# Order of the weight splits, head scalings and key turns in the input projection of a one-core decoder step

## The chip, the cores and the metric

The kernel runs as one program on one core of a Trainium2 chip. The metric is the device time of one execution in microseconds (us), as the median of a few runs. Engines are named as in the profile: PE (matmul), PEld (its weight loads), DVE (VectorE), ACT (ScalarE), POOL (GpSimd), SP (the engine whose queue issues the DMAs).

## The reference, cut to what matters

The reference is one inference step of a two-layer hybrid decoder over 1024 prompt tokens and 64 sample tokens. The change touches only the first stage of layer 0, the combined input projection with what hangs on it:

```
xn = rmsnorm(x, norm_mix[0])
h  = einsum('btd,de->bte', xn, w_in)             # 1088 rows x 3400 columns
qa, ka, va, qi, ki, wi, hb = split(h)
q_a = rmsnorm(qa per head, a_q_norm)             # also k_a and each q_b, k_b
dots = einsum('bqhd,bsd->bqhs', qi, ki) * IDX_DIM**-0.5
sc   = einsum('bqh,bqhs->bqs', wi, relu(dots))   # index scores
_, idx = top_k(sc, 256)                          # the keys that sparse attention sees
```

A head's rmsnorm is a sum of squares, a root, a reciprocal, a product with the reciprocal, and a product with a gain row of 64 values. The bias of every softmax comes from a table of 32 buckets by 20 heads, spread out over distances.

## The kernel before, in words

`stage_project` takes the first 459 us of the 2642 us span. Everything behind it (window attention, sparse attention, output projection, MLP, the recurrent layer, the second MLP) is code that the change does not touch. A block ends with a barrier of all engines, so the next stage begins when the last engine of this one is through.

The 3400 columns are cut into 8 groups (`GROUPS`, L56): group 0 is "kikv" (index keys, index weights, keys, values), 1 "qi" (index queries), 2 "qa", 3 to 5 "qk0" to "qk2", 6 and 7 values. The 1088 rows are 9 tiles (tile 0 is the 64 sample rows). The pair (group, tile) is called a step here, as (3,5). `rows_n` numbers the steps: n = 9 x group + tile.

Each fp32 product is made of three passes over high and low parts. A weight unit is the 128 x 512 piece k of a group (8 to a group). It is loaded by SP into a ring of three raw buffers (`load_w`, L517, waits until the low part three units back is made), its high part is made by a DVE cast (`split_high`, L967), its low part by a POOL subtraction (`split_unit_low`, L612). PE begins a group when all 8 low parts are there (L807).

A tile's way is: PE `project` (L818, three PSUM banks in turn, so PE can be three tiles ahead of ACT); ACT copies the bank to a row buffer, scaled (L748; a ring of three, so the copy of step n waits until the rows of step n-3 have been stored by DMA); ACT squares (L770); DVE sums (L998); ACT root (L695), issued one tile later; DVE reciprocal and product (`norm_apply`, L1014), also a tile later; POOL head gain (L661); SP `store` (L544), two tiles later in its queue. In the groups that aren't stored (1) or not normed (6, 7) steps drop out. Tile 0 of the later groups is projected together with its low part, and POOL adds the two halves (`add_first`, L640).

In group 0 seven tiles are projected together. Behind (1,0) PE makes the bias table (six chunks, L899; the last two need the banks back that ACT takes first), ACT takes it in six copies (`take_table`, L713) when all its copies of group 0 are done, SP writes it to memory (L557, L559) and then writes strips of it (`bias_halves` to `bias_strips`, L564, five of them, the first two of 2 MB), with loads of weights and the stores of (0,7) and (0,8) between them in SP's order. After (1,1) PE turns the index keys by transposes in one PSUM bank, in three parts with an ACT copy between them (L910, L754), then the sample queries (`turn_queries(0)`, L835, which waits for `add_first(1)`), and after (1,4) the queries of tile 2 (`turn_queries(2)`, L839), which wait for ACT's copy of (1,3). Index scores follow, mixed with the projection.

From group 2 on ACT and DVE find the top 256 of each row by bisection over 31 bits, spread over the tile steps: `show` (L292, four ACT sign passes with sums) and `turn` (L303, L310, L312, tiny DVE operations) need each other's results in turn, in 3 of 4 steps. DVE ends with `settle` and `close` (L322 to L359), one piece after the other. The units of groups 3 to 7 stand at fixed steps in `WEIGHTS_AT` (L484 to L489), and DVE, POOL and SP all work down the same list of steps.

## Time and profile before

| | us |
|---|---|
| time, median of 3 runs | 2646.19 (2646.01 to 2652.25) |
| the profiled execution | 2644.74 |
| its span, first to last instruction | 2641.8 |
| PE busy in the span | 2533.1 (96%) |
| DVE, ACT, POOL busy in the span | 1560.0, 1050.5, 1246.4 |
| granted TensorE clock, mean | 0.979 |
| projection stage, end of PE's last matmul to start of the next stage's first | 455.84 to 459.24 |

The busy shares are means over stages with different limits; the projection stage has to be read by its stretches. A wait row says which engine or DMA ended the idle time of an engine.

### The profile page before, as it was taken

To read this page: it belongs to the slowest core of one execution; us is meant where nothing else is said; L and a number is where in the kernel's file an instruction comes from. 1 tells how busy PE (TensorE), PEld (TensorE's weight loads), DVE (VectorE), ACT (ScalarE), POOL (GpSimd) and SP (SyncE) were. 2 spreads that over 40 slices of the span, in tenths; PEclk is the share of its full clock that TensorE was granted. 3 is DMA by queue.
4 is the path that set the end of the run, shared out by engine and by line. 5 is a ranking of instruction groups with operands and counts; after the bars stand their busy time and mean duration, and the time that the engine had idled before them with its cause. 6 is when DMAs were issued, how large, how long until landed. Compare 5 with 4: busy or idle time off the path is not lost.

```text
span 2641.8 us, 44709 instructions
## 1 busy us (share of the span) xinstructions
PE 2533.1 (96%) x16674; PEld 2350.2 (89%) x16674; DVE 1560.0 (59%) x2510; ACT 1050.5 (40%) x1883; POOL 1246.4 (47%) x833
## 2 busy tenths in 40 slices
PE   7999999989879999999999989998999999999998
PEld 6667778866669999999999979998999999999998
DVE  5369886436555555545554697565355645554557
ACT  5358784866532332233223242435222233223322
POOL 4114451017335665556555583323455466545655
PEclk9999999989889999999999999999999999999999
DMA  5402222734461111111111112233111111111112
GB/s 151 137 21 77 82 84 84 233 91 117 152 228 48 41 56 48 40 48 56 48 33 46 48 33 82 75 114 140 43 40 57 40 41 55 48 40 48 56 48 84
DMA packets 109203, 198.71 MB, mean 75 GB/s; under 512 B 22709, under 2 KB 62773, under 8 KB 108805
## 3 DMA queue, kind: packets, MB, share of 16 engines
q1 hardware_dynamic: 104602, 191.85, 23.0%
q10 hardware_dynamic: 4480, 5.27, 0.6%
q8 instruction: 73, 1.20, 0.2%
q14 instruction: 48, 0.39, 0.1%
HBM read 170.97 MB, written 47.17 MB: 83 GB/s over the span
## 4 chain that ended last, share of the span: by engine, by line
PE 66%; DVE 3%; issue 1%; ACT 1%; POOL 1%; DMA 0%; DVEq 0%; ACTq 0%
PE d_ps L2322 40%; PE d_ps L2849 24%; PE d_ps L3211 1%; PE d_ps L2337 1%; DVE rstd_all L2409 0%; DVE x_t L2953 0%; DVE xg_low L3339 0%; DVE x_t L2944 0%; DVE xg_low L2348 0%; POOL m_hidden_low L2692 0%; DVE m_hidden L2897 0%; PE d_ps L2382 0%; DVE unit_high L2305 0%; POOL unit_low L2309 0%; DVE m_shared_part L2944 0%
## 5 line engine op out<-in xcount | busy, mean ns | idle before, releaser
L2322 PE MATMUL d_ps<-xg_high,unit_high 128*128 128x364 f32 (+1 forms) x2112 | 472.6, 332 | 9.0 <-DVE xg_low L3339 3.1
L2322 PE MATMUL d_ps<-xg_high,unit_low 128*128 128x364 f32 (+1 forms) x2112 | 464.8, 328 | 0.0
L2322 PE MATMUL d_ps<-xg_low,unit_high 128*128 128x364 f32 (+1 forms) x2112 | 464.4, 328 | 0.0
L2309 POOL TENSOR_TENSOR unit_low<-unit_raw,unit_high 128x1024 fp32r<-128x1024 f32 x96 | 232.4, 2421 | 412.2 <-DVE unit_high L2305 231.1
L2849 PE MATMUL d_ps<-m_hidden_high,unit_high 128*128 128x272 f32 x1792 | 373.8, 290 | 14.2 <-DVE x_t L2944 8.9
L2322 PEld LDWEIGHTS d_ps<-xg_high,unit_high 128*128 128x128 f32 x2112 | 365.5, 188 | 15.6 <-issue 5.6
L2849 PE MATMUL d_ps<-m_hidden_high,unit_low 128*128 128x272 f32 x1792 | 370.9, 288 | 0.0
L2849 PE MATMUL d_ps<-m_hidden_low,unit_high 128*128 128x272 f32 x1792 | 370.6, 288 | 0.0
L2322 PEld LDWEIGHTS d_ps<-xg_high,unit_low 128*128 128x128 f32 x2112 | 367.0, 189 | 0.0
L2322 PEld LDWEIGHTS d_ps<-xg_low,unit_high 128*128 128x128 f32 x2112 | 365.3, 188 | 0.0
L2699 POOL TENSOR_TENSOR unit_low<-unit_raw,unit_high 128x512 fp32r<-128x512 f32 x128 | 176.8, 1382 | 390.3 <-ACT unit_high L2767 388.9
L2767 ACT ACTIVATE unit_high<-unit_raw 128x512 fp32r<-128x512 f32 x128 | 81.1, 633 | 567.9 <-PE d_ps L2849 358.1
L2944 DVE TENSOR_TENSOR x_t<-x_t,d_ps 128x544 f32<-128x544 f32 x320 | 227.1, 718 | 134.2 <-PE d_ps L2849 133.8
L2849 PEld LDWEIGHTS d_ps<-m_hidden_high,unit_high 128*128 128x128 f32 x1792 | 281.6, 189 | 16.0 <-issue 15.4
L2849 PEld LDWEIGHTS d_ps<-m_hidden_high,unit_low 128*128 128x128 f32 x1792 | 283.6, 189 | 0.0
L2849 PEld LDWEIGHTS d_ps<-m_hidden_low,unit_high 128*128 128x128 f32 x1792 | 281.1, 188 | 0.0
L2692 POOL TENSOR_TENSOR m_hidden_low<-m_hidden,m_hidden_high 128x544 fp32r<-128x544 f32 x160 | 250.8, 1591 | 23.1 <-ACT m_hidden_high L2756 23.1
L2897 DVE SCALAR_TENSOR_TENSOR m_hidden<-d_ps,rstd_all 128x1092 f32<-128x1092 f32 x64 | 82.5, 1292 | 293.8 <-PE d_ps L2322 293.7
L818 PE MATMUL proj_ps<-w_high,x_high 128*128 128x512 f32 (+2 forms) x464 | 178.9, 386 | 2.8 <-ACT rows L748 2.6
L818 PE MATMUL proj_ps<-w_low,x_high 128*128 128x512 f32 (+2 forms) x464 | 175.7, 379 | 0.0
L818 PE MATMUL proj_ps<-w_high,x_low 128*128 128x512 f32 (+2 forms) x464 | 175.4, 378 | 0.0
L2761 ACT ACTIVATE unit_high<-unit_raw 128x1024 fp32r<-128x1024 f32 x60 | 63.6, 1060 | 250.6 <-PE d_ps L2849 127.3
(398 smaller groups left out, 4175.4 us busy)
## 6 DMA issues: line engine op xcount, KB each, us to landing
unit_raw<-w_units SPq DMA_DIRECT2D x160, 512.0 KB, 3.6
unit_raw<-w_in SPq DMA_DIRECT2D x48, 256.0 KB, 2.9
proj_rows<-rows SPq DMA_DIRECT2D x32, 256.0 KB, 2.0
s_win<-win_cache SPq DMA_DIRECT2D x2, 3968.0 KB
proj_rows<-rows SPq DMA_DIRECT2D x36, 128.0 KB, 1.8
sw_rows<-proj_rows SPq DMA_DIRECT2D x12, 384.0 KB, 4.7
select_work<-xt SPq DMA_DIRECT2D x8, 546.0 KB, 3.8
x_t<-xt SPq DMA_DIRECT2D x4, 1092.0 KB, 14.4
```

The source lines that it names most:

```text
L818: last = nc.tensor.matmul(ps[p % 3][:, 0:w], x, y[gi % 2][:, k, 0:w], start=(n == 0), stop=(n == len(passes) - 1))
L2309: self.nc.gpsimd.tensor_tensor(self.wl[slot][:, :], self.raw[:, slot, :], self.wh[slot][:, :].bitcast(F32), ALU.subtract).then_inc(self.w_ ...
L2322: last = self.nc.tensor.matmul(ps[:, c, 0:USED[c]], w[wslot][:, wk], v[:, k, c, 0:USED[c]], start=(k == 0 and n == 0), stop=(k == nk - 1 a ...
L2337: last = self.nc.tensor.matmul(ps[:, c, 0:USED[c]], w[wslot][:, wk], v[:, k, c, 0:USED[c]], start=(k == 0 and n == 0), stop=(k == nk - 1 a ...
L2692: nc.gpsimd.tensor_tensor(hl[:, i, q, :], SOURCES[i], hh[:, i, q, :].bitcast(F32), ALU.subtract).then_inc(h_low, 1)
L2699: nc.gpsimd.tensor_tensor(out, src, top.bitcast(F32), ALU.subtract).then_inc(part_low, 1)
L2761: nc.scalar.activation(d.wh[slot], d.raw[:, slot, :], ACT.Copy).then_inc(d.w_high, 1)
L2767: nc.scalar.activation(part_slots(d.high, x), src, ACT.Copy).then_inc(part_high, 1)
L2849: last = nc.tensor.matmul(out[:, c, :], w[:, i // 4, c0:c0 + P], h[:, i, q, HC * c:HC * (c + 1)], start=(i < 4 and q == 0 and x == 0), sto ...
L2897: nc.vector.scalar_tensor_tensor(out=v[:, t, :].rearrange("p (c n) -> p c n", c=NCH), in0=d.ps[t][:, :, 0:CH], scalar=0.0, in1=d.rstd[:, : ...
L2944: nc.vector.tensor_tensor(out, out, d.quarter[i], ALU.add).then_inc(added, 1)
L3211: last = nc.tensor.matmul(ps[use % 2][:, c, 0:CC], gw[:, n % 2, x, :], cv[:, n % 2, c, :], start=True, stop=True)
```

## The change

Four edits. `WEIGHTS_AT` puts the units k = 0 to 7 of groups 4 to 7 at steps -1, 0, 0, 1, 2, 2, 3, 4 of the group before (it was -1 to 6, one to a step). POOL does a step's low parts first and the head gain of an earlier tile behind them: two tiles behind in group 0, one from group 2 on (it was the gain of the same tile, which waited for DVE, ahead of the next low part). The last two gains of group 0 come at (1,0). One more unit of group 1 is loaded and split ahead (`FIRST_LOADS` 4, `FIRST_SPLITS` 3), which puts its load in SP's queue ahead of the load of the bias selector. The key turns use three PSUM banks and no wait between them; the sample queries are turned, and taken by ACT, one tile later; ACT takes the pending root of (0,8) before the table.

```diff
@@ -435,12 +435,16 @@
             return GROUPS[gi][1]
 
         WAVE = 7
-        FIRST_LOADS = 3
-        FIRST_SPLITS = 2
+        FIRST_LOADS = 4
+        FIRST_SPLITS = 3
 
         def table_bank(c):
 
             return pss[c // 2 % 2][:, 512 * (c % 2):512 * (c % 2) + 512]
+
+        def key_bank(t):
+
+            return pss[t - 1] if t else psx
 
         def bank(p):
 
@@ -486,7 +490,7 @@
             WEIGHTS_AT[k - AHEAD_3].append((3, k))
         for gi in range(4, NGR):
             for k in range(KD):
-                WEIGHTS_AT[NT * (gi - 3) + k - 1].append((gi, k))
+                WEIGHTS_AT[NT * (gi - 3) + (2 * k + 1) // 3 - 1].append((gi, k))
         SHOW_AT = {STEPS[1 + 4 * y // 3]: y for y in range(BITS + 1)}
         KEY_TURNS = [(0, TS + 3 * P), (TS + 3 * P, TS + 7 * P), (TS + 7 * P, TS + 8 * P)]
 
@@ -510,6 +514,7 @@
                 sp.wait_ge(S["filled"], 1)
                 sp.dma_start(relb[0:NBUCKET, :], a["rel_bias"]).then_inc(S["pick_in"], 16)
                 load_w(1, 2)
+                load_w(1, 3)
                 sp.wait_ge(S["x_squared"], KD)
                 sp.wait_ge(S["x_low"], KD)
                 sp.dma_start(pick, a["bias_pick"]).then_inc(S["pick_in"], 16)
@@ -639,27 +644,45 @@
                 v = st[0:TS, n % NST, 0:w]
                 nc.gpsimd.tensor_tensor(v, v, first_low[:, 0:w], ALU.add).then_inc(S["first_sum"], 1)
 
+            def gain_rows(gi, i):
+                for h0, hn, row, _ in kinds(gi):
+                    n = rows_n(gi, i)
+                    pool.wait_ge(S["normed"], NORM_AT[gi, i] + 1)
+                    v = st[:, n % NST, HD * h0:HD * (h0 + hn)].rearrange("p (h d) -> p h d", h=hn)
+                    nc.gpsimd.tensor_tensor(v, v, gains[:, row:row + 1, :].broadcast_to([P, hn, HD]),
+                                            ALU.mult).then_inc(S["gained"], 1)
+
+            def gain_late(gi, i, lag):
+                if NT * gi + i >= lag:
+                    gain_rows(*divmod(NT * gi + i - lag, NT))
+
             for gi in range(NGR):
                 for i in range(NT):
-                    if i == 0 and gi in (1, 2):
-                        add_first(gi)
-                    if i == NT - 1 and 2 <= gi < NGR - 1:
-                        add_first(gi + 1)
                     k = i + (FIRST_SPLITS if gi == 0 else 0)
-                    if gi < 2 and k < KD:
-                        split_unit_low(pool, gi + 1, k)
-                    if gi == 1 and i == NT - 1:
-                        for k in range(AHEAD_3):
-                            split_unit_low(pool, 3, k)
-                    if gi >= 2 and i < NT - 1:
-                        for unit in WEIGHTS_AT[NT * (gi - 2) + i]:
-                            split_unit_low(pool, *unit)
-                    for h0, hn, row, _ in kinds(gi):
-                        n = rows_n(gi, i)
-                        pool.wait_ge(S["normed"], NORM_AT[gi, i] + 1)
-                        v = st[:, n % NST, HD * h0:HD * (h0 + hn)].rearrange("p (h d) -> p h d", h=hn)
-                        nc.gpsimd.tensor_tensor(v, v, gains[:, row:row + 1, :].broadcast_to([P, hn, HD]),
-                                                ALU.mult).then_inc(S["gained"], 1)
+                    if gi == 0:
+                        if k < KD:
+                            split_unit_low(pool, 1, k)
+                        gain_late(0, i, 2)
+                    if gi == 1:
+                        if i == 0:
+                            gain_rows(0, NT - 2)
+                            gain_rows(0, NT - 1)
+                            add_first(1)
+                        if k < KD:
+                            split_unit_low(pool, 2, k)
+                        if i == NT - 1:
+                            for k in range(AHEAD_3):
+                                split_unit_low(pool, 3, k)
+                    if gi >= 2:
+                        if gi == 2 and i == 0:
+                            add_first(2)
+                        if i < NT - 1:
+                            for unit in WEIGHTS_AT[NT * (gi - 2) + i]:
+                                split_unit_low(pool, *unit)
+                        if (gi, i) != (2, 0):
+                            gain_late(gi, i, 1)
+                        if i == NT - 1 and gi < NGR - 1:
+                            add_first(gi + 1)
                 if gi >= 2:
                     for unit in WEIGHTS_AT[NT * (gi - 2) + NT - 1]:
                         split_unit_low(pool, *unit)
@@ -669,6 +692,8 @@
                         v = work[:, WORK_OFF[j] + P * j:WORK_OFF[j] + P * (j + 1)]
                         nc.gpsimd.affine_select(out=v, in_=v, compare_op=ALU.is_ge, fill=MASK, base=0,
                                                 pattern=[[-1, P]], channel_multiplier=1).then_inc(S["masked"], 1)
+
+            gain_rows(NGR - 1, NT - 1)
 
         def take_turn(act, j):
             act.wait_ge(S["turned"], TURN_Q[j])
@@ -718,6 +743,8 @@
                     p = NT * gi + i
                     w = width(gi)
                     if gi == 1 and i == 0:
+                        root(*pending)
+                        pending = None
                         take_table()
                     if gi == 1 and i - 3 in SEL_TILES:
                         for h in range(IH):
@@ -751,8 +778,8 @@
                         if i == 0:
                             for t, (x0, x1) in enumerate(KEY_TURNS):
                                 act.wait_ge(S["turned"], t + 1)
-                                nc.scalar.activation(kit[:, x0:x1], psx[:, 0:x1 - x0], ACT.Copy).then_inc(S["turn_taken"], 1)
-                        if i == 1:
+                                nc.scalar.activation(kit[:, x0:x1], key_bank(t)[:, 0:x1 - x0], ACT.Copy).then_inc(S["turn_taken"], 1)
+                        if i == 2:
                             act.wait_ge(S["turned"], TURN_Q[0])
                             nc.scalar.activation(
                                 qst[:, :, :].rearrange("d b (h t) -> d h b t", t=DT),
@@ -903,11 +930,10 @@
             pe.wait_ge(S["ms_dve"], 1)
             pe.wait_ge(S["tab_out"], 16 * 3)
             for t, (x0, x1) in enumerate(KEY_TURNS):
-                turn_free(t + 1)
                 for i in range(NT):
                     if x0 <= tile_col(i) < x1:
                         r = tile_rows(i)
-                        last = nc.tensor.transpose(psx[:, tile_col(i) - x0:tile_col(i) - x0 + r], kk[0:r, i, 0:P],
+                        last = nc.tensor.transpose(key_bank(t)[:, tile_col(i) - x0:tile_col(i) - x0 + r], kk[0:r, i, 0:P],
                                                    ident[0:r, 0:r])
                 last.then_inc(S["turned"], 1)
             for i in range(1, NT):
@@ -916,7 +942,7 @@
                     continue
                 if i > 1:
                     project(1, i)
-                if i == 1:
+                if i == 2:
                     turn_queries(0)
                 if i - 2 in SEL_TILES:
                     turn_queries(i - 2)
```

## Rows read from the trace of the kernel before

**Rows 1.** Windows: stretch, length; busy PE, PEld, DVE, ACT, POOL; clock; DMA.

```profile
98.00:193.00 95.00, 94.27 (x431) 58.22 (x432) 62.97 (x100) 45.75 (x72) 17.39 (x17) 1.00 0.17 48
193.00:412.00 219.00, 207.21 (x870) 164.74 (x869) 187.72 (x493) 180.76 (x353) 101.22 (x101) 0.98 0.27 82
```

**Rows 2.** Waits of PE, 46 to 98 us: line, releaser, total, times, longest.

```profile
PE proj_ps L818 <- POOL w_low L612: 6.9, 1, 6.9
PE turn_ps L835 <- POOL rows L640: 2.8, 1, 2.8
PE turn_ps L910 <- ACT late L754: 1.3, 2, 0.7
```

**Rows 3.** Windows of PE alone: length, busy, granted clock.

```profile
52.90:57.60 4.70, 4.62 (x11) 0.50 0.23 64
...
74.70:81.50 6.80, 4.21 (x16) 0.50 0.65 227
```

**Rows 4.** Timeline of ACT, 40 to 98 us: start, duration, what, idle before.

```profile
44.80 0.47 ACT L748 ACTIVATE rows<-score_ps,rstd_rows 128x256 f32<-128x256 f32 x1 [4.19 <-DMA proj_rows<-rows]
...
63.51 1.25 ACT L713 ACTIVATE late<-score_ps 20x512 f32<-20x512 f32 x2 [0.27 <-PE score_ps L899]
...
83.75 0.58 ACT L757 ACTIVATE sample_queries_t<-turn_ps 64x512 f32<-64x512 f32 x1
95.73 1.84 ACT L748 ACTIVATE rows<-proj_ps,rstd_rows 128x512 f32<-128x512 f32 x3 [11.40 <-DMA proj_rows<-rows]
```

**Rows 5.** Timeline of SP's queue, 54 to 86 us.

```profile
54.08 0.34 SPq L544 DMA_DIRECT2D proj_rows<-rows  x1
...
64.78 0.36 SPq L557 DMA_DIRECT2D bias_rows<-late  x1
...
85.79 0.52 SPq L544 DMA_DIRECT2D proj_rows<-rows  x1
```

**Rows 6.** Timeline of POOL: the last low part of group 1.

```profile
51.66 1.26 POOL L612 TENSOR_TENSOR w_low<-unit_raw,w_high 128x512 fp32r<-128x512 f32 x1
```

**Rows 7.** DMA issues on the page: KB each, us from issue to landing.

```profile
unit_raw<-w_in SPq DMA_DIRECT2D x48, 256.0 KB, 2.9
...
proj_rows<-rows SPq DMA_DIRECT2D x36, 128.0 KB, 1.8
```

**Rows 8.** Timeline of PE: the queries of tile 2.

```profile
97.05 0.66 PE L839 MATMUL turn_ps<-ident,rows 128*128 128x128 f32 x4 [0.33 <-ACT rows L748]
```

**Rows 9.** Waits of PE (193 to 412 us) for the low parts.

```profile
PE proj_ps L818 <- POOL w_low L612: 9.0, 2, 5.6
```

**Rows 10.** Waits of ACT for its row buffers, 197 to 412 us.

```profile
ACT rows L748 <- DMA proj_rows<-rows: 6.7, 8, 1.3
```

**Rows 11.** Timeline of ACT: the copies of (6,5) and (6,6).

```profile
414.38 0.69 ACT L748 ACTIVATE rows<-proj_ps,rstd_rows 128x512 f32<-128x512 f32 x1 [2.19 <-PE proj_ps L818]
419.95 0.69 ACT L748 ACTIVATE rows<-proj_ps,rstd_rows 128x512 f32<-128x512 f32 x1 [0.56 <-PE proj_ps L818]
```

**Rows 12.** Timeline of POOL: the gain of (5,8), then three low parts.

```profile
395.51 2.13 POOL L661 TENSOR_TENSOR rows<-rows,unit_raw 128x256 f32<-128x256 f32 x2 [0.63 <-DVE rows L1014]
397.61 2.45 POOL L612 TENSOR_TENSOR w_low<-unit_raw,w_high 128x256 fp32r<-128x256 f32 x3
```

**Rows 13.** Timeline of DVE: a cast that waits for its load.

```profile
400.77 0.29 DVE L967 CAST w_high<-unit_raw 128x256 fp32r<-128x256 f32 x1 [2.70 <-DMA unit_raw<-w_in]
```

**Rows 14.** DVE's last operation of the stage, and PE's first of the next.

```profile
457.66 0.69 DVE L359 TENSOR_SCALAR select_work<-late 128x1024 f32<-128x1024 f32 x1
...
459.24 0.63 PE L1631 MATMUL sw_ps_x<-ident,unit_raw 128*128 128x128 f32 x4 [3.40 <-PEq L371]
```

**Rows 15.** Timeline: a low part of POOL and a turn's operations on DVE.

```profile
256.12 1.28 POOL L612 TENSOR_TENSOR w_low<-unit_raw,w_high 128x512 fp32r<-128x512 f32 x1
...
256.21 1.22 DVE L310 TENSOR_SCALAR select_flip<-select_count 128x4 int32<-128x4 int32 x1
...
272.91 0.17 DVE L310 TENSOR_SCALAR select_flip<-select_count 128x4 int32<-128x4 int32 x1
```

## Prediction

> **What bounds the kernel now.** I read the page, then windows, waits and timelines of the projection stage, the only stage touched; all times are from the start of the span. Three limits follow each other in it.
>
> Up to 98 us it is a mixed chain. PE waits 6.9 us for the last low part of group 1, 1.3 us between the key turns and 2.8 us for the summed sample rows [rows 2], and its granted clock stands at 0.50, the 1.2 GHz level, from 52.9 to 57.6 and from 74.7 to 81.5 us [rows 3], each time after PE stood idle or nearly so. Beside it runs a DMA chain. When ACT has taken the table (its last two copies begin at 63.51 [rows 4]), SP writes it at 64.78 and then queues strips and weights, so that the store of (0,8) is issued at 85.79 [rows 5]. ACT's copy of (1,2) waits 11.40 us for that store and begins at 95.73; three copies follow back to back in 1.84 us [rows 4]. At 97.05 PE turns the queries of tile 2, after 0.33 us of waiting for the copy of (1,3) [rows 8]. PE and the DMA chain reach 97 us in a dead heat.
>
> From 98 to 193 us PE is busy for 94.27 of 95.00 us [rows 1]: what PE loses or gains before it reaches the bisection whole.
>
> From 193 to 412 us DVE is busy for 188 and ACT for 181 of 219 us [rows 1], bound to each other by show and turn. PE waits 9.0 us for low parts, at two starts of groups [rows 9], but ACT never waits for PE between 197 and 412 us: its copies stand idle for their row buffers only, 6.7 us [rows 10]. PE is up to three tiles ahead, and its stall is paid from that lead. Only at (6,5) and (6,6) does ACT wait for PE, 2.19 and 0.56 us [rows 11]. DVE ends the stage at 458.35 (its last operation starts at 457.66), and the next stage begins at 459.24 while PE has stood for 3.40 us [rows 14]. So PE's stalls of this part are worth 2.19 + 0.56 = 2.75 us at most, not 9.0.
>
> **The first low parts, group 1.** Now POOL makes the parts of k = 5, 6, 7 ahead of the gains of (0,0), (0,1), (0,2). The load of k = 5 now waits for the part of k = 2, which ends near 37.2, so it is issued near 37.6; with 2.9 us to land [rows 7] and the selector's transfer, now issued behind one more weight load, I take 42. The cast, the part (1.26 us [rows 6]) and the gain follow: gain of (0,0) near 44.2. The store lands 1.8 us later [rows 7], so ACT's copy of (0,3), at 44.80 before [rows 4], starts near 46.3. From it: square, sum, the gain's product, then the cast of k = 7 at 48.1 and its low part 48.6 to 49.9. It ended at 51.66 + 1.26 = 52.92 [rows 6]. PE starts group 1 some 3.0 us earlier.
>
> But the gain of (0,2) now stands behind that part, near 50.3, and each later copy of ACT waits for a store three tiles back. Copies of (0,5) and (0,6): 52.2 and 53.9. SP then issues the eight small loads behind the kiwi store of (0,6), and the store of (0,4) leaves near 57.4, where it left at 54.08 [rows 5]. Copies of (0,7) and (0,8) near 59.2 and 60.8, root of (0,8) 62.3, the table from 62.4. ACT takes it in six copies of about 0.6 (1.25 for two [rows 4]): done near 66.0, where it was 63.51 + 1.25 = 64.76. **Table +1.25 us.** PE's 3.0 us are lost to the two table chunks that need ACT's first copies. Bounds: with the copy of (0,3) at 45.0 the same chain gives -0.5, with 47.4 it gives +2.9.
>
> **The key turns.** Three banks take out the 1.3 us, the earlier root and the later sample queries the 2.8 us [rows 2], and the half clock there costs 4.21 / 2 = 2.1 us of PE [rows 3]. These 6 us are real, but they end in front of the turn of the queries of tile 2. That needs the copy of (1,3), which hangs on the store of (0,8), and SP's chain from table to store (64.76 to 95.7) isn't shortened by any edit: it moves by the +1.25. Moreover ACT takes the sample queries (0.58 us [rows 4]) now between the copies of (1,2) and (1,3): they were taken at 83.75, in a hole. **+0.6 us.** So PE reaches the turn near 91.3, stands some 7 us, and goes on near 98.9.
>
> **The clock behind that hole.** After the 6.9 us hole before, the half clock stayed for the 4.62 us of busy PE in the first window [rows 2, 3], which cost 4.62 / 2 = 2.3 us. The new hole is as long, and behind it lies the stretch where PE is the bound. I take **+2.0 us**; bounds 0 (the clock stays up) and 3.4 (6.8 us at half). Sum up to 193 us: 1.25 + 0.6 + 2.0 = +3.85.
>
> **Groups 2 to 7.** The low parts come early enough, and PE's 9.0 us of waiting turn into waiting for ACT's banks. ACT's last waits for PE go: **-2.75**. Against it, the gain of the last tile of a group now follows three low parts instead of none or one. For (5,8): gain 395.51 to 397.64, then three parts of 2.45 / 3 = 0.8 each [rows 12]; now the parts come first, from about 394.9, and the gain ends near 399.1. Store, the copy of (6,2) and the load of the next two units move with it, and the cast at 400.77 that already waited 2.70 us for its load [rows 13] comes near 402.2, ahead of a turn that ACT waits for: **+1.4** (bounds 0 to 2.1). For (4,8) the same order delays the gain by 1.2 us, of which I let half through: **+0.6** (0 to 1.2). The other two group ends move by under 0.5 us, into waits that exist. Doubled units cost DVE a cast of 0.4 us more in one step and less in another: 0.
>
> **Sum.** 3.85 - 2.75 + 1.4 + 0.6 = +3.1 us. The profiled execution took 2644.74 (span 2641.8), so it would take 2647.8; it lies 1.45 us under the median of the runs, so the median becomes 2646.19 + 3.1 = 2649.3. A difference of under 0.3%, about 8 us, can't be told from none here; this is one.
>
> **A lock between POOL and DVE.** A turn's 128 x 4 operation took 1.22 us when it started 0.09 us behind a low part of POOL, and 0.17 us without one [rows 15]. The change puts low parts directly behind the casts, and the turn is DVE's next operation. The Trainium skill ("SBUF — State Buffer", Who interferes with whom) says that GpSimd and VectorE share one pair of ports by a lock held for a whole instruction, and that issue order decides who is blocked. By that rule the trace agrees, and each part in front of a turn costs a part's length. In the sum I count 0, since before the change the parts ran behind a gain and hit the turns too (as this row shows), and the number of parts is the same.
>
> **Rivals.**
>
> A, the lock decides (slower). Of the eight doubled steps six have a turn; the second part blocks another of its operations. Four have parts of 512 columns, 1.22 - 0.17 = 1.05 us each, two parts of 256, 0.55 each: 5.3 us, if the two steps that lose their part in each group give nothing back. 3.1 + 5.3 = +8.4: 2654.6. For: show and turn are one loop with little idle. Against: DVE still waits for ACT in many steps. It decides when more than a third of the doubled steps pass their delay on.
>
> B, the front doesn't slip. The store of (0,0) lands early (table -0.5), the clock stays up or the strips run faster, and groups 6 and 7 keep their 2.75: -0.5 + 0.6 - 2.75 = -2.65: 2643.5. For: landing times are the softest numbers of my chain. Against: the store of (0,4) has SP's eight loads ahead in any case.
>
> C, PE was the bound of the whole stage after all (faster). If groups 2 to 7 alone pay it, the 9.0 us of waits go and, behind each of the two holes, at most the 2.3 us of half clock that the first hole cost: -13.6, 2632.6. With the front's 6.9 + 1.3 + 2.8 it would be -24.6. Against it stand ACT's copies that never wait for PE [rows 10].
>
> D, the edits do not do what they say: PE still waits for low parts of group 4, since casts of DVE are late. Then the -2.75 is missing: 2652.
>
> **How the numbers follow.** Forecast with D and its bounds (-0.5 to +7): 0.56. B: 0.24. A: 0.13. C: 0.07. Faster by over 0.3% is C and the rim of B: 0.09. Slower by over 0.3%: about two thirds of A and the case in which late landing (+2.9), clock (+3.4) and stalls (+3.3) meet: 0.13. The rest, 0.78, is within. Range: from B's far side, 2641, to just over A, 2657. The forecast's own range is 2645.5 to 2653.
>
> **What would show it.** Right: no PE wait for low parts from group 2 on; PE group 1 starts near 50; the table's last copy near 65; the store of (0,8) as many us behind it as before; an idle PE of 5 us or more in front of L839 near 98, with half clock behind it; ACT's waits for PE at (6,5) and (6,6) gone; a DVE cast that waits near 402. Wrong: a table before 64, no hole in front of the queries of tile 2, ACT waiting for PE between 200 and 400 us, or a DVE end more than 3 us before 458.

## The result: 9 us slower, of which the prediction had 3

The changed kernel took 2658.82 us (median of 8 runs, 2656.01 to 2663.64), the kernel before beside it 2652.69 (8 runs, 2646.01 to 2653.60). The ratio is 1.0034, 95% interval 1.0021 to 1.0048: 9.0 us, 5.6 to 12.7. Forecast were +3.1 us and 2649.3, with a range up to 2657.0. The sign was right; the size and the range were not. The base moved too: in five later jobs the kernel before had medians of 2648.84 to 2650.92 where the three runs of the prediction had 2646.19. On that base the measured 9.0 us would have given 2655.2, inside the range.

One profile of each kernel isn't enough here, because the kernel before alone differs from execution to execution. So each was profiled four times. Mean of four (lowest to highest), us from the start of the span:

| | before | after | difference | forecast |
|---|---|---|---|---|
| PE starts group 1 | 52.40 | 50.79 | -1.61 | -3.0 |
| ACT's table done | 65.70 (63.94 to 67.12) | 66.87 (66.50 to 67.41) | +1.17 | +1.25 |
| copy (1,2) to copy (1,3) | 0.58 | 1.06 | +0.48 | +0.6 |
| PE turns the queries of tile 2 | 98.46 (96.27 to 100.34) | 99.87 (99.54 to 100.58) | +1.41 | +1.85 |
| from there to ACT's copy (1,5) | 11.61 (11.57 to 11.65) | 14.45 (14.18 to 14.92) | +2.84 | +2.0 |
| copy (1,5) to the first show | 84.43 (84.40 to 84.47) | 88.26 (84.44 to 89.58) | +3.83 | 0 |
| first show to DVE's end | 265.11 (264.41 to 266.30) | 266.76 (266.65 to 267.02) | +1.65 | -0.75 |
| DVE's end to the next stage | 0.86 | 0.33 | -0.53 | 0 |
| start of the next stage | 460.47 | 469.67 | +9.20 | +3.1 |
| from there to the end of the span | 2187.6 | 2188.2 | +0.6 | 0 |

The 9.20 us at the start of the next stage agree with the 9.0 us of the ratio. The last row is code that the change doesn't touch, and it varies from 2182.5 to 2193.7 us between executions of either kernel: a single profile's span says nothing about 9 us. The table, too, is done at one of two times in the kernel before, near 64 (64.75 and 63.94) or near 67 (67.12 and 66.97), so the differences of means in the upper rows rest on how many of each kind the four were. The profile of after that was taken with the timed runs has a span of 2653.1 us, its execution 2656.01.

Its page: busy times of the engines.

```profile
PE 2542.2 (96%) x16674; PEld 2354.5 (89%) x16674; DVE 1567.5 (59%) x2510; ACT 1049.5 (40%) x1883; POOL 1242.8 (47%) x833
```

PE's waits of 46 to 99.8 us, answering [rows 2] (releaser; total, times, longest):

```profile
PE turn_ps L866 <- ACT rows L775: 6.5, 1, 6.5
PE proj_ps L845 <- POOL w_low L617: 4.1, 1, 4.1
PE score_ps L926 <- ACT late L738: 2.4, 1, 2.4
PE proj_ps L845 <- ACT rows L775: 1.0, 1, 1.0
```

The wait for the low part shrank from 6.9 to 4.1 us, those for the key turns and the summed sample rows are gone, and in their place stands the hole of 6.5 us ahead of the queries of tile 2.

The chain that made it, ACT's timeline after, answering [rows 4]:

```profile
47.17 0.47 ACT L775 ACTIVATE rows<-score_ps,rstd_rows 128x256 f32<-128x256 f32 x1 [3.85 <-DMA proj_rows<-rows]
...
66.12 0.52 ACT L738 ACTIVATE late<-score_ps 20x432 f32<-20x432 f32 x1 [0.85 <-PE score_ps L926]
...
97.93 0.69 ACT L775 ACTIVATE rows<-proj_ps,rstd_rows 128x512 f32<-128x512 f32 x1 [10.61 <-DMA proj_rows<-rows]
98.51 0.58 ACT L784 ACTIVATE sample_queries_t<-turn_ps 64x512 f32<-64x512 f32 x1
98.99 1.25 ACT L775 ACTIVATE rows<-proj_ps,rstd_rows 128x512 f32<-128x512 f32 x2
```

SP's queue after, answering [rows 5]: table, strips and weights still stand ahead of the stores of (0,7) at 75.13 and (0,8) at 88.64. Two of these instructions hold the queue for 3.70 and 9.10 us. The order isn't all of it: the store of (0,8) is seen as landed only at 97.84, 9.2 us after its issue, where such stores take 1.8 us at the median [rows 7].

```profile
66.66 0.36 SPq L562 DMA_DIRECT2D bias_rows<-late  x1
67.06 1.58 SPq L564 DMA_DIRECT2D bias_halves<-late  x2
70.51 0.78 SPq L569 DMA_DIRECT2D bias_strips<-bias_halves  x1
71.33 3.70 SPq L526 DMA_DIRECT2D unit_raw<-w_in  x1
75.13 0.67 SPq L549 DMA_DIRECT2D proj_rows<-rows  x1
76.78 1.80 SPq L537 DMA_DIRECT2D page_keys_t<-kidx_t  x2
78.62 0.76 SPq L569 DMA_DIRECT2D bias_strips<-bias_halves  x1
79.42 9.10 SPq L526 DMA_DIRECT2D unit_raw<-w_in  x1
88.64 0.53 SPq L549 DMA_DIRECT2D proj_rows<-rows  x1
```

PE after, answering [rows 8], and windows of PE (stretch, length; busy; granted clock, DMA share, GB/s), first the stretch behind the hole, then the one that nothing in the prediction had:

```profile
99.71 1.12 PE L866 MATMUL turn_ps<-ident,rows 128*128 128x128 f32 x4 [6.50 <-ACT rows L775]
```

```profile
96.40:106.60 10.20, 6.20 (x16) 0.50 0.47 146
181.80:195.50 13.70, 13.70 (x47) 0.50 0.15 39
```

The second stretch at the 1.2 GHz level lies over the sample scores (the index scores of the 64 sample rows), 64-row products without a wait of PE in front of them. They begin at 177.66 at full clock and end at 190.94; the clock falls in their midst, at 181.8. It holds back DVE, which stands until they are done. DVE in the kernel before, then after:

```profile
181.26 0.42 DVE L1069 COPY sample_work<-turn_ps 64x264 f32<-64x264 f32 x1 [6.18 <-PE turn_ps L932]
181.71 0.16 DVE L1071 TENSOR_TENSOR sample_work<-sample_work,later_mask 64x8 f32<-64x8 f32 x1
```

```profile
190.98 0.42 DVE L1095 COPY sample_work<-turn_ps 64x264 f32<-64x264 f32 x1 [10.40 <-PE turn_ps L958]
191.44 0.93 DVE L1097 TENSOR_TENSOR sample_work<-sample_work,later_mask 64x8 f32<-64x8 f32 x1
```

Between them lie 9.7 us: 5.5 were there at copy (1,5), the rest is this stretch. The operation behind the copy then took 0.93 us in place of 0.16, since it meets POOL's 1.27 us of adding rows, which began at 191.07 and ended at 192.34. In another execution of the same changed kernel neither is seen: there the copy waits 6.18 us again and the operation takes 0.16.

```profile
187.09 0.42 DVE L1095 COPY sample_work<-turn_ps 64x264 f32<-64x264 f32 x1 [6.18 <-PE turn_ps L958]
187.54 0.16 DVE L1097 TENSOR_TENSOR sample_work<-sample_work,later_mask 64x8 f32<-64x8 f32 x1
```

### The profile page after: what moved, and what is told of

It reads as the page before. It is cut to its first block, busy times and chain, and to the rows that moved or that the text cites. A ratio compares the mean times of both kernels' runs of the same rounds, so it can differ in the third digit from the quotient of the medians.

```text
span 2653.1 us, 44709 instructions
## 1 busy us (share of the span) xinstructions
PE 2542.2 (96%) x16674; PEld 2354.5 (89%) x16674; DVE 1567.5 (59%) x2510; ACT 1049.5 (40%) x1883; POOL 1242.8 (47%) x833
## 3 DMA queue, kind: packets, MB, share of 16 engines
HBM read 170.97 MB, written 47.17 MB: 82 GB/s over the span
## 4 chain that ended last, share of the span: by engine, by line
PE 66%; DVE 3%; issue 1%; ACT 1%; POOL 0%; DMA 0%; DVEq 0%; ACTq 0%
PE d_ps L2348 40%; PE d_ps L2875 24%; PE d_ps L3237 1%; PE d_ps L2363 1%; DVE rstd_all L2435 0%; DVE x_t L2979 0%; DVE x_t L2970 0%; DVE xg_low L3365 0%; DVE xg_low L2374 0%; DVE m_hidden L2923 0%; PE d_ps L2408 0%; DVE m_shared_part L2970 0%; DVE unit_high L2331 0%; POOL unit_low L2335 0%; DMA mixed_low<-mixed_t 0%
## 6 DMA issues: line engine op xcount, KB each, us to landing
x_t<-xt SPq DMA_DIRECT2D x4, 1092.0 KB, 14.2
```

## Experiments

"Half clock in the sample scores" below is the stretch just shown; its mark is the wait of DVE's copy, 10 us and more with it and 6.2 without. The kernel before that stood beside the runs of a job had a median of 2650.32 (e1 to e6), 2650.92 (e7, e8), 2648.84 (e9 to e12), 2650.72 (e13 to e16) and 2650.60 (e17, e18).

**The three parts one by one.** e1 keeps of the change only the groups' weights and late gains from group 2 on, e2 only the order of group 0, e3 only the key turns:

```diff
 e1, e2: as before
-                return pss[t - 1] if t else psx
+                return psx              # and turn_free(t + 1), root behind the table, queries at i == 1
 e1, e3: as before
-        FIRST_LOADS = 4; FIRST_SPLITS = 3; load_w(1, 3); gain_late(0, i, 2)
+        FIRST_LOADS = 3; FIRST_SPLITS = 2; gain_rows(0, i)
 e2, e3: as before
-                WEIGHTS_AT[NT * (gi - 3) + (2 * k + 1) // 3 - 1].append((gi, k))
+                WEIGHTS_AT[NT * (gi - 3) + k - 1].append((gi, k))   # and gain_rows(gi, i) in place of gain_late
```

> The kernel before with one part of the change only: from group 2 on, the units at 3 per two tiles and POOL's low parts ahead of the head gains of a tile before. My theory (the front costs, the back is nearly free because ACT and DVE pace it): PE's two waits for low parts of 9.0 us go, the first show starts at 193 us as before, settle begins within 2 us of 425.6 and DVE ends within 2 us of 458.3; time +0 to +2 us against before. Rival (the lock and the bunched parts slow the show and turn loop): first show at 193, but DVE ends 5 us or more later. Second rival (PE was the bound): DVE ends 5 us or more earlier, time -5 to -13.

> The kernel before with the order of group 0 only: four loads and three splits ahead, gains two tiles behind the low parts. My theory: PE starts group 1 near 50.7 instead of 53.0, but ACT's table copies end near 66.6 (64.8 before), SP's store of (0,8) and the copy of (1,2) come 2 us later (near 98), so PE turns the queries of tile 2 near 98.8 behind a hole of about 3 to 4 us; it loses 2 us there and up to 2 us of half clock behind the hole: +2 to +4 us at 120 us. Rival (the earlier low parts are a gain as they stand): PE passes 97 us on or before its time, time -2 us or better.

> The kernel before with the key turns in three banks, the root of (0,8) ahead of the table and the sample queries a tile later. My theory: PE's waits of 4.1 us and most of the half clock near 75 to 81 us go, but the copy of (1,2) still begins at 95.7, so a hole of about 5 us opens in front of the turn of the queries of tile 2, which comes at 97.5 (0.5 for the sample queries taken between the copies), with half clock behind it: +0.5 to +3.5 us at 120 us. Rival (the waits removed are on the path): PE is 4 us or more earlier at 97 us, time -4 us or better.

Measured: e1 2653.32 us, ratio 1.0011 (0.9998 to 1.0024); e2 2654.15, 1.0012 (0.9996 to 1.0027); e3 2658.39, 1.0036 (1.0022 to 1.0050). In e1 PE waits for no low part from group 2 on, only 10.0 us for ACT's rows, and the kernel isn't faster. In e2 the expected hole of 3 to 4 us didn't come: PE reaches the queries of tile 2 at 98.17 without waiting. The key turns alone are as slow as the whole change. In e3's profile the hole stands, though its table was done at 63.91, and 14.85 us go from the queries of tile 2 to copy (1,5) where e1 and e2 have 11.65. Windows of these stretches in e3 and in e2 show why:

```profile
97.00:111.90 14.90, 14.20 (x50) 0.73 0.45 132
```

```profile
98.20:109.80 11.60, 10.77 (x51) 1.00 0.45 123
```

The same work takes 3.3 us longer at a mean clock of 0.73. What PE gained ahead of the hole it didn't keep. Rival C, PE as the bound throughout, falls: e1 takes out the waits of groups 2 to 7 and e3 those of the key turns, and neither is faster.

**The stores ahead of the table.** e4 is the changed kernel with the stores of (0,7) and (0,8) issued by SP before it waits for the table; e8 moves three loads of group 2 ahead of it as well. e9 has the key turns alone with e4's stores.

```diff
                 if gi == 1 and i == 0:
+                    store(0, NT - 2)
+                    store(0, NT - 1)
+                    for k in range(3): load_w(2, k)      # e8 only
                     sp.wait_ge(S["tab_sb"], NTC)
```

> The changed kernel, with the stores of (0,7) and (0,8) issued in SP's queue ahead of the wait for the table instead of behind the strips. My theory (the hole of 6.5 us is the DMA queue's): copies of (1,1), (1,2), (1,3) no longer wait for DMA, PE turns the queries of tile 2 near 93 instead of 99.7 with no hole and full clock; but the second weight unit of group 2 lands near 97.5, so DVE's first scores start near 98 to 99 instead of 103.7. 4 to 8 us faster than the changed kernel up to 170 us. Rival (the hole belongs to something else, PE or ACT): the hole stays, time unchanged against the changed kernel. On the half clock of 181.8 to 195.5 us, in the sample scores: if it is a chance of phase, it stays in some of these four runs and not in others; if the change brings it, it stands in none of the first three.

> The changed kernel with the stores of (0,7) and (0,8) and the first three loads of group 2 issued ahead of the wait for the table. Against the kernel with the stores alone moved (turn of the queries at 92.4, but the copy of (1,5) at 105.6, 13.2 us behind it, since DVE's scores wait for the second unit): DVE's scores start with the first relu near 95, the copy of (1,5) comes near 104, 1 to 2 us earlier; first show near 189.5. Time 5 to 8 us under the changed kernel in its own fast runs, 1 to 3 under the kernel before. Rival (DMA isn't what the scores wait for): as with the stores alone.

> The kernel before with the change's edits to the key turns (three banks, the root early, the sample queries of tile 2 later) and the two stores of tile 7 and 8 of the first groups issued ahead of SP's wait for the table; the weights' parts and gains of the groups stay where they were before, and so does the order of the first group's projections. If the time of the change comes from the hole ahead of the queries of tile 2 and the half clock that follows it, and from the work that the weights' parts add at the end of the loop, this kernel has neither: no hole there, the queries of tile 2 near 92 us in place of 97 to 100, copy (1,5) near 105, and the median 2 to 5 us below the kernel before (2646 to 2649, ratio 0.998 to 0.9993). If the half clock in the sample scores comes with the key turns themselves, it shows here too (copy of the sample scores near 184 or later) and the time is that of the kernel before within 1 us.

Measured: e4 2650.39 us, 0.9996 (0.9983 to 1.0008); e8 2651.72, 1.0010 (0.9991 to 1.0029); e9 2646.11, 0.9984 (0.9967 to 1.0001). SP in e4:

```profile
65.86 0.99 SPq L549 DMA_DIRECT2D proj_rows<-rows  x2
66.97 0.35 SPq L564 DMA_DIRECT2D bias_rows<-late  x1
```

With them ACT copies (1,2) at 80.68 in place of 97.93, and PE meets the queries of tile 2 without waiting, in e4 and in e9:

```profile
92.38 0.60 PE L868 MATMUL turn_ps<-ident,rows 128*128 128x128 f32 x4
```

```profile
93.39 0.60 PE L862 MATMUL turn_ps<-ident,rows 128*128 128x128 f32 x4
```

Between after and e4 two stores moved, and the ratio fell from 1.0034 to 0.9996, 10 us; between e3 and e9 the same two, and it fell from 1.0036 to 0.9984, some 14 us, each ratio known to about 4 us. That is the clearest result of the study: the edits bring PE to the queries of tile 2 some 5 us earlier, near 93 us, and with the stores behind the table that is lost again. The profiles account for the 10 us and not for the 14: the next stage begins at 457.90 in e4, 11.8 us before the mean of after, and at 463.40 in e9, 3.4 us before e3's 466.77; e9's profile had half clock in the sample scores. What the two stores alone do to the kernel before was not run. e8's loads added nothing that the times show, against the 1 to 3 us under the kernel before that were expected; copy (1,5) came at 104.67, where e4 has 105.61, and the half clock stood in its sample scores. e9's interval lies wholly under the changed kernel's, but it reaches 1.0001, so it isn't shown to beat the kernel before.

**The hole filled.** e7 puts 24 unread products into it, so that PE works where it stood.

```diff
+                if i == 4:
+                    for n in range(24):
+                        nc.tensor.matmul(pss[n % 2][:, 0:512], xh[:, n % KD, 0:P], wh[1][:, n % KD, 0:512],
+                                         start=True, stop=True)
                 if i - 2 in SEL_TILES:
                     turn_queries(i - 2)
```

> The changed kernel with 24 matmuls of 512 columns, whose results nobody reads, in the hole before the queries of tile 2 (24 x 0.233 = 5.6 of the 6.5 us). My theory: the turn of the queries stays at 99.7 +/-0.7, but the clock stays at full behind it, so the copy of (1,5) comes 12.0 us behind the turn instead of 14.4: 2.5 to 3 us faster at 115 us, and in the whole, or 6 to 9 us with the sample scores if the half clock there comes from the hole too. Rival (the clock behind the hole doesn't matter, or the fillers delay PE): same or slower than the changed kernel.

Measured: 2657.75 us, 1.0024 (1.0012 to 1.0037). 1.20 us of the hole stayed, and the stretch behind it took 13.1 us at a mean clock of 0.87: of the 2.8 us about half came back. The ratio lies 2.6 us under the changed kernel's, which the intervals can't tell from nothing. The half clock in the sample scores was there all the same, so it doesn't need the full idle time of the hole.

**Repeats.** e5, e12 and e15 are the kernel before again, e6, e10 and e16 the changed one, e11 is e3, one profile each.

> The kernel before, profiled a second time. Theory (the half clock in the sample scores near 172 to 181 us depends on the state in which PE arrives, which the hole near 98 us changes only by shifting the phase): sample scores at full clock here in most executions, 9.1 us from their first matmul to the copy of the result (181.26 in the first profile, +/-1.5), show at 193. Rival (pure chance, the same for every kernel): as likely to stand at half here as in the changed kernel, and then the copy comes at 185 or later.

> The changed kernel, profiled a second time. The hole before the queries of tile 2 is 6 to 7 us again and the half clock stands behind it for 6 us or more. The half clock in the sample scores (13.7 us in the first profile): my theory expects it again, since all eight executions were 2656 us or more and the price of the hole with its clock alone explains 5.5 of 9 us; the rival (chance) has it gone in this profile, and DVE's copy of the sample scores then comes near 187 instead of 190.98.

> The changed kernel once more, for one profile. If the stretch at half clock in the sample scores comes in some executions only, it comes here or not, and the hole of 6.4 us ahead of the queries of tile 2 and about 14.5 us from there to copy (1,5) stand in any case. Without that stretch the first show is near 199, with it near 203.

> The key turns alone once more, for one profile: the hole of 6.5 us and about 14.9 us behind it to copy (1,5) again; last show to the end of VectorE's work some 1.3 us shorter than in the changed kernel. If the stretch at half clock in the sample scores belongs to the key turns, it shows again (first show near 200); if it comes by execution it may be gone (first show near 197).

> The kernel before once more, for one profile: no hole, 11.6 us from the queries of tile 2 to copy (1,5), and, if the half clock in the sample scores comes with the hole or the key turns, full clock there as in both profiles of it so far; if it comes by execution whatever the kernel, it may show here.

Measured: 2656.96, 2660.30, 2659.52, 2655.90, 2651.86 us, and 2648.06 (e15) and 2665.83 (e16). The hole of 6.2 to 6.5 us and its 14.2 to 14.9 us behind it stood in each of after, 5.0 and 13.5 in e11, and in none of before. Half clock in the sample scores: before 0 of 4, after 3 of 4 (not e6), e3 and e11 both.

**The moment of the sample scores.** After e12 it had been seen in 7 of 9 profiles of kernels with the new key turns (after, e3, e7, e8, e9, e10, e11; not e4, e6) and in none of 5 without (before three times, e1, e2). e13 and e14 only push what follows 1.6 us back, in the changed kernel and in the kernel before, e17 in e9:

```diff
+                if gi == 1 and i == 8 and piece == 0:
+                    for n in range(7):
+                        x, y, k = passes[0]
+                        nc.tensor.matmul(ps[p % 3][:, 0:w], x, y[gi % 2][:, k, 0:w], start=True, stop=True)
                 for n in range(each * piece, each * (piece + 1)):
```

> The changed kernel with the first product of the projection (1,8) computed seven times more into its own bank, overwritten each time: PE has 1.6 us more to do near 155 us, the same number results, and all that follows begins 1.6 us later. If the half clock in the sample scores comes from the moment at which these small products begin, the later moment falls where kernels without it had theirs: the first show is near 202 in place of 203 to 204 in spite of the added work, and the median 1 to 3 us below the changed kernel (ratio to before 1.002 to 1.003). If it belongs to the key turns and what they leave behind, it stands as before and the kernel is 1.6 us slower than the changed one: first show near 205, ratio 1.004 to 1.005.

> The kernel before with the same seven repeated products in (1,8). If the moment decides, the sample scores of this kernel now fall where the clock drops: half clock in them, 4 to 5 us more than the 8.67 us they take, and with the added 1.6 us a median 4 to 6 us above the kernel before (ratio 1.0015 to 1.0025). If it belongs to the key turns, none is seen here and the kernel is slower by the 1.6 us alone (1.0006).

> The kernel before once more, for one profile. If the moment alone decides and the kernel before mostly meets the good one, full clock in the sample scores again (8.67 us from the first to the last of their small products' stretch).

> The changed kernel once more, for one profile: the hole of 6.4 us and some 3 us of clock behind it in any case; the half clock in the sample scores in two of three executions, if it goes on as in the three so far.

> The kernel of e9 (the kernel before with the new key turns and the two stores ahead of the table) with the seven repeated products in (1,8). In e9's profile the sample scores stood at half clock (first show 195.98). If the moment decides, they begin 1.6 us later here and at full clock: first show near 193 to 194 in spite of the added work, and the median 1 to 4 us under e9's: 2642 to 2645, ratio 0.997 to 0.998. If not: first show 197.6, median 1.6 us above e9's, ratio 0.999.

Measured: e13 2657.23 us, 1.0038 (1.0021 to 1.0054); e14 2656.21, 1.0017 (1.0002 to 1.0032); e17 2651.73, 1.0008 (0.9997 to 1.0019). DVE's copy in e13, e14 and e17:

```profile
188.32 0.42 DVE L1099 COPY sample_work<-turn_ps 64x264 f32<-64x264 f32 x1 [6.18 <-PE turn_ps L962]
```

```profile
189.85 0.42 DVE L1073 COPY sample_work<-turn_ps 64x264 f32<-64x264 f32 x1 [10.26 <-PE turn_ps L936]
```

```profile
181.45 0.42 DVE L1095 COPY sample_work<-turn_ps 64x264 f32<-64x264 f32 x1 [9.99 <-PE turn_ps L958]
```

In the profiles e13 lost the half clock and e14, an otherwise unchanged kernel before, got it. So no edit of the change is needed for it, nor does one force it (e6). With all 20 profiles it was seen in 9 of 13 with the new key turns and in 1 of 7 without: whether the key turns make it likelier is not settled by so few. But the two timed expectations fare differently: e14's median is 5.5 us up, inside the 4 to 6 expected, while e13's isn't under the changed kernel's at all. In e17 the half clock came again, against the expectation, and the median rose by more than the added 1.6 us; that its first show came at 194.04, as expected, is no support, since its table was done at 63.87 where e9's was done at 67.06. A shift of 1.6 us isn't a remedy. What in an execution decides where the clock falls stays open.

**The last loop.** e18 is e4 with the weights' parts and gains of groups 2 to 7 as before (the third part of the first diff).

> The changed kernel with the stores of (0,7) and (0,8) ahead of the table, and with the weights' parts and the gains of groups 2 to 7 where they were before. Against e4, which differs by these alone: if they cost in the loop what the profiles show, 1.5 us less from the first show to the end of VectorE's work (265.3 in place of 266.8) and the median 1 us under e4's ratio of 0.9996 (0.999). If their gain at (6,5) and (6,6) of 2.75 us held, as the prediction had it, this kernel would be the slower one by 1 to 2 us (1.000).

Measured: 2651.70 us, 0.9993 (0.9979 to 1.0007): 0.8 us under e4's ratio, which the intervals can't tell from nothing. From the first show to DVE's end it took 266.59 us, as long as e4 (266.58) and not the 265.3 expected: a miss. Over all profiles the nine with the edit lie at 266.3 to 267.9, mean 266.7, the eleven without (this one among them) at 264.4 to 266.6, mean 265.5. So 1.3 us is the mean, not the difference of each pair.

## Why the prediction was wrong, step by step

**What held.** The reading of the bound did: the front's gains end at the DMA chain. The table's +1.25 was +1.17 as a difference of means, in part by luck: against the 64.76 that it was worked out from, the four tables of after are 1.7 to 2.7 us later. The sample queries' +0.6 was +0.48, the hole of 5 us or more with half clock behind it stands, and at copy (1,5) the sum of +3.85 was +4.25. That only PE's start of group 1 came 1.6 and not 3.0 us earlier cost nothing, as it is lost to the table chunks anyway (2.4 us of waiting at L926). The copy of (0,3) came at 47.17, near the upper bound (47.4) and not at 46.3. e4 and e9 show the cause of the hole by experiment.

**The clock behind the hole** was mis-sized: +2.0 was taken from the first hole, +2.84 measured, inside the bounds of 0 to 3.4. The half clock lasted from 96.4 to 106.6 us, with 6.20 us of busy PE in it, where the first window of [rows 3] has 4.62.

**"From 98 to 193 us PE is busy: what PE loses or gains before it reaches the bisection whole."** This is the step that failed. It took the 94.27 us of [rows 1] to be worth the same at whatever moment they start. They hold a stretch of 64-row products at which the clock fell in 10 of 20 profiles and not in the other 10. Windows of these products in before and in after:

```profile
172.10:181.00 8.90, 8.55 (x65) 1.00 0.24 62
```

```profile
177.60:190.60 13.00, 12.66 (x65) 0.66 0.16 42
```

From the start of the first to the end of the last, the 64 products take 9.05 us at full clock and 12.7 to 14.2 where it fell, and DVE's copy waits 3.7 to 5.2 us longer. The price is these 3.7 to 5.2 us of PE and 0.77 us of DVE. In the four and four profiles it makes 3.83 of the 9.20 us. How much of the timed 9.0 us it makes is less sure: e13, in whose one profile it is absent, wasn't faster. So the step is shown to fail in the profiles; its share of the time, and why the clock falls in one execution and not in another, stay open.

**Groups 2 to 7** have the wrong sign: +1.1 with the stage's end (1.65 - 0.53) where -0.75 stood. The -0.53 goes with this edit: from DVE's end to the next stage it is 0.32 to 0.33 us in all nine profiles with it, 0.79 to 0.88 in the eleven without. The waits went as said. PE waits for no low part, only for ACT's rows; ACT waits for PE no longer at (6,5) and (6,6), copied at 426.04 and 431.50 (two in the first row). After, answering [rows 9], [rows 11] and [rows 12]:

```profile
PE proj_ps L845 <- ACT rows L775: 9.8, 9, 2.0
```

```profile
426.04 1.24 ACT L775 ACTIVATE rows<-proj_ps,rstd_rows 128x512 f32<-128x512 f32 x2
431.50 0.67 ACT L775 ACTIVATE rows<-proj_ps,rstd_rows 128x512 f32<-128x512 f32 x1
```

```profile
407.41 2.58 POOL L617 TENSOR_TENSOR w_low<-unit_raw,w_high 128x256 fp32r<-128x256 f32 x3
409.95 1.43 POOL L652 TENSOR_TENSOR rows<-rows,unit_raw 128x256 f32<-128x256 f32 x2
```

But the -2.75 isn't found at the end of the loop. ACT's waits in it, without those for POOL's rows, which are 7.2 us in both, in before:

```profile
ACT late L292 <- DVE select_minus_bound L312: 16.3, 13, 2.2
...
ACT rows L748 <- DMA proj_rows<-rows: 6.7, 8, 1.3
ACT rows L748 <- PE proj_ps L818: 2.8, 2, 2.2
ACT head_roots L695 <- DVE head_means L1003: 1.4, 5, 0.6
```

and after:

```profile
ACT late L292 <- DVE select_minus_bound L312: 18.6, 13, 3.1
ACT rows L775 <- DMA proj_rows<-rows: 8.3, 7, 2.5
...
ACT head_roots L720 <- DVE head_means L1029: 2.1, 3, 1.4
```

-2.8 for PE, +2.3 and +0.7 for DVE, +1.6 for row buffers: +1.8, beside the loop's +1.65 (1.38 between these two profiles). A tally of waits doesn't prove that each of them sets the loop's length. e4 (18.5, 8.2 and 2.1, none for PE) against e18 (15.7, 5.6 and 1.1, and 6.7 for PE in four waits) shows the same exchange by this one edit; e18's longer waits for PE go with a loop that was no shorter than e4's. The +1.6 for row buffers is of the size of the +1.4 and +0.6 that late gains were to cost; the +3.0 for DVE was not in the sum.

**The lock (rival A)** was half right, and not in the turns. Groups of DVE from the first show to the last, in before:

```profile
L1014 DVE TENSOR_TENSOR rows<-rows,head_inverse 128x512 f32<-128x512 f32 x36 | 25.8, 718 | 1.2
...
L303 DVE TENSOR_TENSOR select_count<-select_signs,select_level 128x4 f32<-128x4 f32 x32 | 16.3, 510 | 26.6 <-ACT late L292 26.0
L967 DVE CAST w_high<-unit_raw 128x512 fp32r<-128x512 f32 x28 | 12.8, 458 | 0.5 <-DMA unit_raw<-w_in 0.5
...
L1003 DVE TENSOR_SCALAR head_means<-head_sums 128x4 f32<-128x4 f32 x54 | 6.9, 174 | 0.9
```

and after (busy, mean ns, idle before):

```profile
L1040 DVE TENSOR_TENSOR rows<-rows,head_inverse 128x512 f32<-128x512 f32 x36 | 27.2, 757 | 1.2
...
L993 DVE CAST w_high<-unit_raw 128x512 fp32r<-128x512 f32 x28 | 15.9, 584 | 0.4 <-DMA unit_raw<-w_in 0.4
L303 DVE TENSOR_TENSOR select_count<-select_signs,select_level 128x4 f32<-128x4 f32 x32 | 11.7, 364 | 24.1 <-ACT late L292 23.4
L1029 DVE TENSOR_SCALAR head_means<-head_sums 128x4 f32<-128x4 f32 x54 | 9.3, 217 | 0.9
```

Casts, head means and scalings cost 3.1 + 2.4 + 1.4 = 6.9 us more, the turns' counts 4.6 us less. Between e18 and e4, which differ by this edit alone, the means are the same: casts 452 and 593 ns, head means 175 and 217, scalings 718 and 757, counts 511 and 363. The likely reason, argued from the order of the edit and not tested by itself, is that POOL's parts were moved from in front of the counts to in front of the casts and the scalings. The rival's "two doubled parts give nothing back" was wrong (4.6 us came back), and the main sum's "number of parts is the same, so 0" was wrong by about 2 us. "SBUF — State Buffer" of the Trainium skill, Who interferes with whom, has the rule that the order of issue decides who is blocked; the rows agree with it in that the price moved with the order. Rival A's sum of +8.4 lies near the measured 9.0 by luck: the loop lost 1.65 us, and 8.1 us came ahead of it. The +1.4 for (5,8) can't be singled out: three parts ran ahead of its gain and a cast waited 1.55 us for its load near 414, against 2.70 before [rows 13].

**The chances.** B to D don't apply: the front slipped, PE wasn't the bound, the edits did what they say. The forecast's own range of 2645.5 to 2653 was built from the bounds of terms that it had; a term that it lacked, seen in 3 of the changed kernel's 4 profiles, stood outside. The time lies beyond the wider range also because the base rose by 6.5 us.

## What to carry to other kernels

Follow the queue that issues the stores before speeding up an engine: in the changed kernels, two stores issued ahead of a wait that they don't need were worth 10 to 14 us, and without them what the edits gained for PE ended in a hole and the half clock behind it. Where a stretch of small products stands on the critical path, take several profiles of each kernel before a difference of some us is explained, and compare marks within the stage, not spans. A wait that disappears can be replaced by waits for another engine, as here on ACT (6.7 us for PE less, 6.4 us for DVE and row buffers more, e18 to e4), and work moved on one engine can change the durations of another (DVE's casts 452 to 593 ns).

## What the runs showed of the hardware that was not expected

- The granted clock fell to the 1.2 GHz level over 64-row products (64x128, 64x8 and 64x264 f32) that PE issued back to back, busy 12.66 of 13.00 us, in 10 of 20 profiles, in the changed kernel both ways. They took 9.05 us at full clock and 12.7 to 14.2 where it fell.
- The unchanged code behind the stage took 2182.5 to 2193.7 us in eight executions.
- A DVE operation of 64x8 took 0.93 us beside POOL's 64x512 addition and 0.16 without.
- SP was held for 3.70 and 9.10 us by weight loads that it issued behind the first and the second strip of 2048 KB; a store of rows took it 0.34 to 0.67 us. The store of 128 KB behind the second of them landed 9.2 us after its issue, against 1.8 us at the median.
